# Norms over the channels: squares summed as columns with the tokens on partitions

## The reference, cut to what matters

```python
def _rmsnorm(x, g):                       # and _rmsnorm_2, the same without the modulation behind it
    y = x * lax.rsqrt(jnp.mean(x * x, axis=-1, keepdims=True) + 1e-6)
    return y * g

# first block, layers 0 and 1:  h = rmsnorm(x, norm1_g) * (1 + scale) + shift  -> mixers -> x = x + gate * mix
#                               h = rmsnorm(x, norm2_g) * (1 + scale) + shift  -> dense / expert feed-forward
# second block, layers 0 and 1: h = rmsnorm(x, norm1_g_2) -> mixers;  h = rmsnorm(x, norm2_g_2) -> conv feed-forward
```

## Time and profile before

| | us |
|---|---|
| timed runs (3) | 2860.03, 2868.94, 2869.28 |
| median | 2868.94 |
| span of the profiled execution | 2861.5 |
| PE busy | 2699.6 (94%) |
| DVE busy | 1932.5 (68%) |
| ACT busy | 1475.9 (52%) |
| POOL busy | 104.8 (4%) |

### The profile page before, as it was taken

How to read it: one execution, slowest core, us unless ns; L and a number is a source line. 1 busy time by engine, 2 the same in 40 slices (tenths; PEclk the granted TensorE clock), 3 DMA queues, 4 the chain that set the end, 5 groups by cost and what they waited for, 6 DMA issues and landing times.

```text
span 2861.5 us, 50422 instructions
## 1 busy us (share of the span) xinstructions
PE 2699.6 (94%) x21334; PEld 2275.9 (80%) x21334; DVE 1932.5 (68%) x2291; ACT 1475.9 (52%) x1748; POOL 104.8 (4%) x74
## 2 busy tenths in 40 slices
PE   6998898999999978789999999999999899989999
PEld 4875776888778768678888888888888779988999
DVE  3365866322444767578898989888898667666766
ACT  3345243212333533367777777777777445454544
POOL 1100000000013000010000000000000000000000
PEclk9999999999999989899999999999999999999999
DMA  8514101322225240089999999999998334542453
GB/s 321 230 59 181 66 3 59 110 96 97 95 90 203 76 156 4 3 339 361 339 368 340 360 345 353 359 339 368 357 359 345 151 118 175 181 159 94 165 189 118
DMA packets 81803, 581.79 MB, mean 203 GB/s; under 512 B 9272, under 2 KB 11072, under 8 KB 11840
## 3 DMA queue, kind: packets, MB, share of 16 engines
q1 hardware_dynamic: 78336, 571.48, 53.1%
q10 hardware_dynamic: 3264, 7.33, 0.7%
HBM read 577.73 MB, written 1.05 MB: 202 GB/s over the span
## 4 chain that ended last, share of the span: by engine, by line
PE 83%; DVE 8%; ACT 4%; issue 2%; DMA 1%; PEldq 1%; POOL 0%; DVEq 0%; POOLq 0%; ACTq 0%; PEld 0%; SPq 0%
PE banks L2522 21%; PE banks L2548 11%; PE banks L2900 9%; PE banks L1077 9%; PE banks L857 8%; PE banks L1103 4%; PE banks L891 4%; PE banks L1534 3%; PE banks L3250 2%; PE banks L2097 1%; DVE ring_split L307 1%; PE banks L522 1%; PE banks L2532 1%; DMA ring<-parts 1%; PE banks L2936 1%
## 5 line engine op out<-in xcount | busy, mean ns | idle before, releaser
L2729 DVE TENSOR_TENSOR ring_split<-ring,arena_split 128x2048 fp32r<-128x2048 f32 x336 | 770.0, 2293 | 113.6 <-ACT arena_split L2641 105.9
L2641 ACT ACTIVATE arena_split<-ring 128x2048 fp32r<-128x2048 f32 x336 | 644.4, 1919 | 57.7 <-PE banks L2548 57.6
L307 DVE TENSOR_TENSOR ring_split<-ring,arena_split 128x2048 fp32r<-128x2048 f32 x140 | 321.3, 2295 | 322.9 <-ACT arena_split L301 322.9
L301 ACT ACTIVATE arena_split<-ring 128x2048 fp32r<-128x2048 f32 x142 | 270.8, 1908 | 98.0 <-PE banks L1077 74.0
L2522 PE MATMUL banks<-arena_split 128*128 128x512 f32 x896 | 301.3, 399 | 6.6 <-DVE ring_split L2729 6.6
L2548 PE MATMUL banks<-arena_split 128*128 128x512 f32 x896 | 297.3, 392 | 7.3 <-DVE arena_split L2760 7.2
L2522 PE MATMUL banks<-arena_split,mix_split 128*128 128x512 f32 x896 | 303.7, 401 | 0.0
L2548 PEld LDWEIGHTS banks<-arena_split 128*128 128x128 f32 x896 | 168.2, 188 | 50.0 <-issue 10.8
L2522 PEld LDWEIGHTS banks<-arena_split 128*128 128x128 f32 x896 | 169.7, 189 | 42.2 <-DVE ring_split L2729 7.0
L857 PE MATMUL banks<-mix_split,ring_split 128*128 128x256 f32 x704 | 199.0, 283 | 0.0
L857 PE MATMUL banks<-h_split,arena_split 128*128 128x256 f32 x704 | 197.6, 281 | 0.0
(11 more groups left out here) (419 smaller groups left out, 5403.3 us busy)
## 6 DMA issues: line engine op xcount, KB each, us to landing
ring<-parts SPq DMA_DIRECT2D x541, 1024.0 KB, 4.8
arena<-bias ACTq DMA_DIRECT2D x2, 2048.0 KB, 8.9
x_buf<-xt SPq DMA_DIRECT2D x1, 2048.0 KB, 7.9
constants<-con SPq DMA_DIRECT2D x1, 1952.0 KB, 14.6
out<-x_buf ACTq DMA_DIRECT2D x4, 256.0 KB, 2.2
arena<-lora ACTq DMA_DIRECT2D x2, 256.0 KB, 5.1
arena<-gate ACTq DMA_DIRECT2D x2, 256.0 KB, 5.3
arena<-sgw ACTq DMA_DIRECT2D x2, 256.0 KB
```

The lines of the kernel that those rows point to most:

```text
L301: act.activation(high[:, m % depth, :], slots[:, n % RING, :], ACT.Copy).then_inc(w_high.h, w_high.one(times))
L307: dve.tensor_tensor(low_slots[:, n % RING, :], slots[:, n % RING, :], high[:, m % high.shape[1], :].bitcast(F32), ALU.subtract).then_inc(w ...
L2641: act.activation(high[:, m % 3, :], slots[:, m % RING, :], ACT.Copy).then_inc(wh_ok.h, 1)
L2729: dve.tensor_tensor(low_slots[:, m % RING, :], slots[:, m % RING, :], high[:, m % 3, :].bitcast(F32), ALU.subtract).then_inc(wl_ok.h, 1)
```

## The change

The norms' sums are turned round. `product` takes a block of 128 tokens' squares (128 channels x 128 tokens) as the stationary operand and one column of `mean_d` as the moving one. The mean of a token then stands in one column per block with the tokens on the partitions: 4 columns for 512 tokens, 2 for 256. The root and the reciprocal work on these columns. `spread_out` brings the inverse back over all partitions: for each block a product whose stationary operand is the column of inverses, broadcast to 128 x 128, and whose moving operand is `ident`; the result stands in a bank of PSUM, and `scale` reads it there. POOL's fold is gone, all eight tiles are summed by PE, and where `sum` did nothing for k below 5 it now runs products. `spread_out` is placed behind the fourth modulation half in norms 1 and 3 and at the start of PE's work in the others. `ident` moves into the first load of the constants. In the conv feed-forward the zero products and PE's wait for the first memset go, the memset moves behind the norm's work on DVE, and the first down product of each bank starts it.

```diff
-for _name, _n in [("mean_d", 128), ("eps", 8), ("iota", 8), ("head_sum", 128), ("ident", 128), ("eye64", 64), ("mask_zr", 512),
+for _name, _n in [("mean_d", 128), ("eps", 8), ("iota", 8), ("ident", 128), ("head_sum", 128), ("eye64", 64), ("mask_zr", 512),
...
-        def fold(self, pool):
-
-            pool.wait_ge(self.squared.h, self.squared.at(1))
-            for k in range(1, self.FOLDED):
-                pool.wait_ge(self.squared.h, self.squared.at(k + 1))
-                if k > 1:
-                    pool.wait_ge(self.added.h, self.added.at(k - 1))
-                pool.tensor_tensor(self.sq[:, 0, :], self.sq[:, 0, :], self.sq[:, k, :], ALU.add)\
-                    .then_inc(self.added.h, self.added.one())
-
         def sum(self, pe, k):
-            if self.folded:
-                if k < self.FOLDED - 1:
-                    return
-                if k == self.FOLDED - 1:
-                    pe.wait_ge(self.added.h, self.added.at(self.FOLDED - 1))
-                    self.product(pe, 0, True, False)
-                    return
             pe.wait_ge(self.squared.h, self.squared.at(k + 1))
             self.product(pe, k, k == 0, k == KT - 1)
...
         def product(self, pe, k, start, stop):
-            mm = pe.matmul(bank(MEAN)[:, 0:self.hi - self.lo], C("mean_d"), self.sq[:, k, :], start=start, stop=stop)
+            last = self.blocks - 1
+            for b in range(self.blocks):
+                mm = pe.matmul(bank(MEAN)[:, b:b + 1], self.sq[:, k, b * P:(b + 1) * P], C("mean_d")[:, 0:1],
+                               start=start and b == 0, stop=stop and b == last, skip_group_check=True)
...
         def take_root(self, act):
-            n = self.stat.hi - self.stat.lo
+            n = self.stat.blocks
             act.activation(root[:, 0:n], bank(MEAN)[:, 0:n], ACT.Sqrt, bias=eps(EPS_RMS)).then_inc(self.rooted.h, self.rooted.one())
 
         def invert(self, dve):
-            r = root[:, self.cols[0] - self.stat.lo:self.cols[1] - self.stat.lo]
+            n = self.stat.blocks
             dve.wait_ge(self.rooted.h, self.rooted.at(1))
-            dve.reciprocal(r, r).then_inc(self.inverse.h, self.inverse.one())
-            dve.wait_ge(self.inverse.h, self.inverse.at(self.nth + 1))
+            dve.reciprocal(root[:, 4:4 + n], root[:, 0:n]).then_inc(self.inverse.h, self.inverse.one())
+            dve.wait_ge(self.spread.h, self.spread.at(1))
+
+        def spread_out(self, pe):
+
+            pe.wait_ge(self.inverse.h, self.inverse.at(1))
+            for b in range(self.stat.blocks):
+                mm = pe.matmul(bank(self.spread_bank)[:, b * P:(b + 1) * P], root[:, 4 + b:5 + b].broadcast_to((P, P)), C("ident"),
+                               start=True, stop=True)
+            mm.then_inc(self.spread.h, self.spread.one())
...
-                ins = dve.scalar_tensor_tensor(dst[:, k, c], xT[:, k, c], self.gain(k, s), root[:, r], ALU.mult, ALU.mult)
+                ins = dve.scalar_tensor_tensor(dst[:, k, c], xT[:, k, c], self.gain(k, s), bank(self.spread_bank)[:, r],
+                                               ALU.mult, ALU.mult)
...
-            for _ in range(2 * mod.n):
+            for i in range(2 * mod.n):
                 mod.half(pe)
+                if i == 3:
+                    normed.spread_out(pe)
...
             def opening():
-                pe.wait_ge(ac.h, ac.at(1))
+                tokens.spread_out(pe)
...
-                        for w, h in ((wh, hid_high), (wh, hid_low), (wl, hid_high)):
+                        for g, (w, h) in enumerate(((wh, hid_high), (wh, hid_low), (wl, hid_high))):
                             mm = pe.matmul(y(t), w[:, j, t * P:(t + 1) * P], h[:, U % 2, j * 256:(j + 1) * 256],
-                                           start=False, stop=False, skip_group_check=True)
+                                           start=U == 0 and j == 0 and t % 2 == 0 and g == 0, stop=False, skip_group_check=True)
...
-            pe.wait_ge(ac.h, ac.at(1))
-            for b in range(4):
-                pe.matmul(bank(4 + b), C("ident"), hid[:, 0, :], start=True, stop=False, skip_group_check=True)
             opening()
...
             if stat:
-                stat.sums(pe)
+                for k in range(KT):
+                    stat.sum(pe, k)
...
+            tokens.on_dve(dve)
             for j in range(2):
                 dve.memset(hid[:, j, :], 0.0).then_inc(ac.h, ac.one())
-            if tokens:
-                tokens.on_dve(dve)
             split(2, None, 1)
```

More of the change, by code:

```diff
@@ L349, in build, with __init__ @@
     class Squares:
-        FOLDED = KT - 2
-        def __init__(self, cols, at, buf=None, folded=True):
+        def __init__(self, cols, at, buf=None):
             self.lo, self.hi = cols
-            self.folded, self.added = folded, S("x_squares_added")
+            self.blocks = (self.hi - self.lo) // P
             self.sq = (Arena(at) if buf is None else Arena(at, buf, KT * T)).take(KT * (self.hi - self.lo), KT)
@@ L405, in build, with __init__ @@
     class Normed:
-        def __init__(self, stat, cols, gain, shift, nth=0):
-            self.inverted = False
+        def __init__(self, stat, cols, gain, shift, nth=0, spread_bank=0):
+            self.inverted, self.spread_bank, self.spread = False, spread_bank, S("norm_spread")
             self.stat, self.gain, self.shift, self.nth = stat, gain, shift, nth
@@ L784, in _ @@
                     ahead.split_low(dve)
-        @block.gpsimd
-        def _(pool):
-            stat.fold(pool)
         end_phase()
@@ L1030, in feed_forward @@
         stream["got"] += 3 * N
-        if stat:
-            @block.gpsimd
-            def _(pool):
-                stat.fold(pool)
         end_phase()
@@ L2951, in values @@
                 mm.then_inc(o_ok.h, o_ok.one())
-            for _ in range(4 * front):
+            for i in range(4 * front):
                 mod.half(pe)
+                if i == 3:
+                    tokens.spread_out(pe)
             for kk in range(KT):
@@ L3680, in __init__, with spread_out @@
             self.half_high, self.half_low = S("first_half_high"), S("first_half_low")
+        def spread_out(self, pe):
+            pass
         def scale(self, dve, k, dst):
@@ L3747, in build @@
     lat = (CTX, T)
-    stat = Squares((0, T), 0, folded=False)
-    entry = lambda l, stat: Normed(stat, (0, T), gain1(l), lambda t, s: modc(l, t, s))
+    stat = Squares((0, T), 0)
+    entry = lambda l, stat: Normed(stat, (0, T), gain1(l), lambda t, s: modc(l, t, s), spread_bank=4)
     tokens = entry(0, stat)
@@ L3766, in build @@
         if l:
-            second_mixers(l, Normed(stat, lat, lambda k, s, l=l: Q2(l, "norm1_g", k), None), None)
+            second_mixers(l, Normed(stat, lat, lambda k, s, l=l: Q2(l, "norm1_g", k), None, spread_bank=3), None)
         else:
@@ L3770, in build @@
         stat = out_project(lat, ff_high("conv"))
-        normed = Normed(stat, lat, lambda k, s, l=l: Q2(l, "norm2_g", k), None)
+        normed = Normed(stat, lat, lambda k, s, l=l: Q2(l, "norm2_g", k), None, spread_bank=3)
         stat = Squares(lat, 18432) if l < DEPTH - 1 else None
```

6 lines of the change are left out of this document (removed).

## The result

The changed kernel takes 2888.34 us (median of 4 runs, 2885.02 to 2890.43), the kernel before 2867.80 (4 runs). The ratio is 1.0073, 95% interval 1.0058 to 1.0088: slower by 20.5 us where 11.4 were forecast. In the profiled executions the spans are 2884.4 and 2861.5. The direction was right, and the time lies just inside the range, 0.7 us from its upper end. The size was not right: the sum held little more than half of the loss. That the time is inside at all is partly luck: the forecast's own range ended at 2885, and the part up to 2889 was there for rival (c), which is not what cost the time (norms 2 and 4 lose 2.2 and 0.4 us, where (c) had some 5 and 2.5 on top of the forecast). With 25, 18 and 11 runs in the later comparisons, the kernel before is at 2867.8, 2869.0 and 2867.5.

A forecast was written before the change was run, and what follows sets the result against it. PE was taken to bound the kernel (busy 94% of the span, 83% of the chain). Per-norm terms 6.8 + 2.0 + 3.5 + 0.3 + 1.4 - 2.6 = +11.4 us on 2868.9 gave 2880.3, range 2866 to 2889.

The forecast's parts named there:

- rival (c): Narrow products between the tiles pull the tiles to half clock, about +5 and +2.5: +19, 2888 us; chance 0.13.
- Norm 1: Kernel's start, 512 columns: 64 narrow records stay at half clock, sums end at 29.5 us instead of 24.6; +6.8 us.
- Norm 2: Ahead of the wide feed-forward, 512 columns: sums +3.5, chain -2.4, clock +0.9; +2.0 us (0 to +4).
- Norm 3: Ahead of the second mixers, 512 columns: interleaved sums +2.6, end +0.8, chain -0.9, clock +1.0; +3.5 us (+1 to +6.5).
- halves or spread at half, 0 to 2.5, taken 1.0: Clock term of Norm 3: modulation halves or the spread run at half clock; +1.0 us, bounds 0 to 2.5.
- 4.1 becomes about 3.3, -0.9: Chain term of Norm 3: root and reciprocal hide behind four halves, the spread does not; -0.9 us with the hand-over.
- Norms 5 and 7: Ahead of conv feed-forwards: sums +0.75, chain 2.85 to 1.3, opening's half clock 1.6; +0.7 us each (-1.1 to +2.2).
- Norm 6: Behind the first conv feed-forward, 256 columns: sums -2.3, chain -1.0, clock +0.7; -2.6 us (-3.5 to -1).
- Norm 4: Ahead of the experts, 256 columns: sums +0.8, chain -1.0, clock +0.5; +0.3 us (-0.5 to +1.5).
- (a): Narrow products do hold the clock up, at the start and in all norms: about -1.5, 2867.4 us; chance 0.17.
- (b): The start's delay is taken back because loads run ahead of PE meanwhile: +4.6, 2873.5 us; chance 0.06.
- (d): A narrow record is cheaper than 0.11 us everywhere; at 0.08 the total is zero; chance 0.04.

The follow-up runs named there:

- 128-column kernel: Changed kernel with every product of the squares moving 128 equal columns of the constant in place of one; 2866.74 us, ratio 1.0002 to the kernel before.
- eight wide sums: Kernel before without GpSimd's adding: norms 2 to 7 take eight wide products each; 2877.22 us, ratio 1.0032 to the kernel before.
- filled openings: Changed kernel with four products over 256 columns put ahead of the spreading of norms 5 and 7; 2883.46 us, ratio 1.0054 to the kernel before.

## Why the prediction was partly right

- Norm 1: right in mechanism and nearly in size (7.9 for 6.8). The sums end at 29.4 for 29.5, and ACT's copies behind the first four and the next four halves come 6.5 and 7.4 us late; the second has the spread ahead of it, which was to be hidden. The last copy is 6.9 us late, and then ACT waits 1.04 us for a load. Where that wait is missing, in four of the experiments that leave norm 1 as in after, the norm costs 6.3 to 6.6.
- Norm 2: 2.2 (and 1.9) for 2.0, its chain 2.64 for "1.8 to 2.7".
- Norm 3 is the step that failed: 7.9 for 3.5, of which two terms of the sum hold 4.4.
  - The first is the clock, "halves or spread at half, 0 to 2.5, taken 1.0". What after loses there beyond the 128-column kernel is 4.2: up to the root 4.8 against 3.4 (3.4 was forecast, so the number of products was priced right; in the first profile this part is the longer pause, in the second half clock on the last tile), and from the root to L2873 10.5 against 7.7 (1.7 for the halves, 0.9 for the spread, 0.2 for L490 between them). The upper end was nearer, and the row to take it from was there: L522's 3.64 in the earlier trace rows, also behind narrow work. That the clock would cost something ahead of the root was not in the sum.
  - The second is "4.1 becomes about 3.3, -0.9". The scaling did come sooner behind the root (3.3 us with 128 columns), but the row of the next stage did not: from the root to that row it is 7.4 us before and 7.7 with 128 columns. The row waits for ACT's copy behind the eighth half, and the spread stands ahead of the last four halves and pushes that copy. The gain was taken on a wait that did not end last.
- Norms 5 and 7: 1.5 and 1.6 for 0.7 each. The opening of norm 5 starts 0.8 us sooner relative to before, for 1.0, and then loses 2.3 for 1.6, being at half for 5.2 us and not 3.3. The printed terms, 1.76 + 1.76 - 1.1 - 1.56 for the sums, 2.85 to 1.3 for the chain and 1.6 for the clock, give +0.9 and not +0.7. That the zero products had held the clock is only half of the cause; the narrow sums ahead let it fall.
- Norm 6: -1.8 for -2.6. "The sums end within 1.5 us of the last square" was wrong (2.4), since the last of 32 records run at half.
- Norm 4: right (0.4 and 0.8 for 0.3).
- The missing term is the second mixer, +3.4. The sum took the clock only next to the sums. The stretches there stand behind small work of the mixer that every kernel has. With 128 columns everywhere they are gone; with 128 columns in norms 4 to 7 alone the third is left; with eight wide sums the third is left too; in the kernel with filled openings, whose sums are narrow, two of them went. So they also depend on where work falls in time, and what in particular ties them to the sums stays open.
- The rivals: (a) is out for the change and close to exact for its 128-column form. (b) is out by the kernel with norm 1 alone undone. (d) is out: 0.11 to 0.13 us in every full-clock group. (c) was named for norms 2 and 4 and did not happen there in after's profile. What it describes did happen in norm 3. In the second profile of after one half-clock stretch lies at 860.6 to 864.0, around the last tile, and three of the experiments have one in the same place (856.1, 859.3 and 863.3). There it costs what the longer pause costs in the first profile.

## What to carry over

When wide products are replaced by many that move one or a few columns, price the clock first and the columns later: here a record of one column took as long as one of 128, and with 128 columns the loss was gone. Before a shorter chain is put down as a gain, look which wait ends last there; in norm 3 it was another one. And a stretch at half clock cost nothing in norm 3 where TensorE went at DVE's pace, and much where its own work was dense. Where a narrow moving operand is padded for free, as 128 equal columns of a constant were, pad it, and check the lengths of the wide work behind it. And a reduction that another engine did in otherwise idle time is worth keeping when its replacement stands in the order of the engine that bounds the kernel.

## What was not expected of the hardware

- At the start, 64 back-to-back records of one or 32 columns kept half-clock lengths (0.215 us each) for 13.8 us of uninterrupted work; with 128 columns they took 9.0.
- A record that moves 128 columns of f32 takes no longer than one that moves a single column (0.12 us each in norm 3).
- Norm 3's opening ran at 0.50 before and at 1.00 after, with DVE busy all the time, and took the same time.
- The clock column of the windows reads 1.00 in the first 30 us while the records have half-clock length.
- Runs of one kernel spread by 12 us (before, 2863.5 to 2875.4 in 25 runs), along with their mean clock (0.977 at the slowest, 0.982 at the fastest).
